# A head's mean taken out of the recurrence's values while they are turned into rows

## What is computed

```python
def rwkv7_scan(r, w, k, v, a, b):
    def step(state, inp):
        r_t, w_t, k_t, v_t, a_t, b_t = inp
        sa = jnp.einsum('bhvk,bhk->bhv', state, a_t)
        state = (state * w_t[:, :, None, :]
                 + sa[..., None] * b_t[:, :, None, :]
                 + v_t[..., None] * k_t[:, :, None, :])
        return state, jnp.einsum('bhvk,bhk->bhv', state, r_t)
...
    y = rwkv7_scan(r, decay, k, v, -kk, kk * a)
    mu = jnp.mean(y, axis=-1, keepdims=True)
    var = jnp.mean(jnp.square(y - mu), axis=-1, keepdims=True)
    y = ((y - mu) * lax.rsqrt(var + GN_EPS)).reshape(bsz, s, c) * gn_w + gn_b
    bonus = jnp.sum(r * k * r_k, axis=-1, keepdims=True) * v
    return (y + bonus.reshape(bsz, s, c)) * g
```

## Time and profile before

| | |
|---|---|
| median of 3 runs | 2821.63 us (2818.89 to 2824.79) |
| the profiled execution | 2820.33 us, span of its profile 2818.5 us |
| PE busy | 2771.2 us, 98% of the span |
| PEld / DVE / ACT / POOL busy | 2434.1 / 2023.7 / 1364.0 / 479.3 us |
| chain that ended last | PE 90%, DVE 5%, ACT 2%, POOL 1% of the span |
| granted TensorE clock | 0.997 of full speed |
| DMA | 474.65 MB, mean 168 GB/s |

### The profile page before, as it was taken

One profiled execution on the slowest core, in us unless ns is written; L12 is line 12 of the kernel. 1 busy time (PEld: TensorE's weight loads), 2 busy tenths in 40 slices (PEclk: granted clock), 3 DMA queues, 4 the chain that ended last, 5 costly groups with the idle time before them and its releaser, 6 DMA issues.

```text
span 2818.5 us, 42260 instructions
## 1 busy us (share of the span) xinstructions
PE 2771.2 (98%) x16660; PEld 2434.1 (86%) x16660; DVE 2023.7 (72%) x3102; ACT 1364.0 (48%) x2051; POOL 479.3 (17%) x526
## 2 busy tenths in 40 slices
PE   8999999999999999999999999999999999999998
PEld 7888888888888888888888888878998888888887
DVE  7987797776776666656657888878677777667655
ACT  6453455455555445434435545434454444444434
POOL 2211011110111111001102635421111111001101
PEclk9999999999999999999999999999999999999999
DMA  6444333455555555555556534221365555555555
GB/s 227 162 160 159 121 116 132 145 191 188 193 187 190 192 191 191 192 190 193 188 183 199 177 124 133 92 76 53 120 202 191 191 192 189 193 188 194 189 180 164
DMA packets 133396, 474.65 MB, mean 168 GB/s; under 512 B 14800, under 2 KB 15056, under 8 KB 132944
## 3 DMA queue, kind: packets, MB, share of 16 engines
q1 hardware_dynamic: 133200, 471.96, 50.3%
HBM read 469.80 MB, written 2.10 MB: 167 GB/s over the span
## 4 chain that ended last, share of the span: by engine, by line
PE 90%; DVE 5%; ACT 2%; POOL 1%; issue 1%; DMA 0%; SPq 0%; DVEq 0%; ACTq 0%; POOLq 0%
PE ps L899 90%; DVE U L1869 1%; DVE ringl L1869 1%; POOL U L2551 1%; ACT high L1409 1%; PE ps L902 1%; POOL U L2624 0%; ACT U L1409 0%; DVE U L1878 0%; DVE xT L1869 0%; DMA xT<-in_x_dram 0%; DVE hx L1869 0%; DVE U L2067 0%; ACT hr L1409 0%; DVE U L1875 0%
## 5 line engine op out<-in xcount | busy, mean ns | idle before, releaser
L899 PE MATMUL ps<-hr,high 128*128 128x512 f32 x4672 | 1491.4, 397 | 11.8 <-DVE ringl L1869 10.8
L1869 DVE TENSOR_TENSOR ringl<-ring,high 128x1024 fp32r<-128x1024 f32 x888 | 1082.6, 1221 | 435.1 <-ACT high L1409 434.6
L1409 ACT ACTIVATE high<-ring 128x1024 fp32r<-128x1024 f32 x888 | 915.6, 1033 | 601.6 <-PE ps L899 590.7
L899 PEld LDWEIGHTS ps<-hr,ringl 128*128 128x128 f32 x4672 | 879.2, 188 | 192.5 <-issue 1.4
L899 PE MATMUL ps<-hr,ringl 128*128 128x256 f32 x4672 | 924.3, 279 | 0.0
L899 PEld LDWEIGHTS ps<-hr,high 128*128 128x128 f32 x4672 | 717.6, 188 | 21.0 <-issue 15.1
L899 PE MATMUL ps<-yur,high 128*128 128x512 f32 (+1 forms) x2432 | 682.9, 370 | 3.8 <-DVE xT L1869 2.2
L2551 POOL TENSOR_TENSOR U<-U,rs 128x256 f32<-128x256 f32 x292 | 264.5, 906 | 1688.3 <-DVE U L1869 1668.8
L899 PEld LDWEIGHTS ps<-yur,ringl 128*128 128x128 f32 x2176 | 400.0, 188 | 79.6
L1409 ACT ACTIVATE U<-ps 128x256 f32<-128x256 f32 (+3 forms) x481 | 172.8, 371 | 592.0 <-PE ps L899 567.6
L899 PE MATMUL ps<-yur,ringl 128*128 128x256 f32 x2176 | 429.9, 279 | 0.0
(11 more groups left out here) (178 smaller groups left out, 1250.2 us busy)
## 6 DMA issues: line engine op xcount, KB each, us to landing
ring<-in_w_dram SPq DMA_DIRECT2D x862, 512.0 KB, 3.3
ring<-in_w_dram SPq DMA_DIRECT2D x48, 256.0 KB, 3.3
xT<-in_x_dram SPq DMA_DIRECT2D x3, 512.0 KB, 8.1
out_dram<-hx SPq DMA_DIRECT2D x3, 512.0 KB, 2.7
cst<-in_cst_dram SPq DMA_DIRECT2D x1, 1374.5 KB, 12.5
yT<-in_lora_dram SPq DMA_DIRECT2D x1, 1024.0 KB, 7.4
xT<-in_x_dram SPq DMA_DIRECT2D x2, 256.0 KB, 4.5
U<-in_lora_dram SPq DMA_DIRECT2D x1, 512.0 KB, 5.4
```

What stands on the lines that cost most here:

```text
L899: return e.matmul(out, l, r, start=start, stop=stop)
L1409: return e.activation(out, i, ACT.Copy, scale=scale)
L1869: return e.tensor_tensor(out, a, b, op)
```

## The change

`cen` is a new constant of 128 columns: the identity less 1/64 on the two 64x64 blocks on the diagonal. In the rows step, v's two chunks are multiplied by `cen` as the moving side instead of transposed, which gives rows with the mean over each head's 64 channels taken out; B's and K's rows are made with transposes instead of with matmuls. ACT squares each chunk of the result directly from PSUM, then copies it. The step `mean` is gone on TensorE, ACT and DVE. In `RECUR` the step `mean` goes and the ACT cost of `o0` and `o1` is 0.6 instead of 0.35. Each stream takes one PSUM bank fewer per q.

```diff
--- before.py
+++ after.py
@@ -50,9 +50,9 @@
          ("kk", ("PE", 0.45), ("DVE", 0.42), ("ACT", 1.7)), ("nrm", ("DVE", 3.1)), ("em", ("DVE", 1.2)), ("exp", ("ACT", 2.9)),
          ("rk", ("PE", 0.45), ("DVE", 0.42)), ("ar", ("DVE", 1.8)), ("rows", ("PE", 0.9), ("ACT", 1.1)),
          ("p1", ("PE", 0.9), ("DVE", 1.4)), ("p2", ("PE", 0.9), ("+DVE", 1.4))] + INVERSE \
-    + [("G0", ("PE", 0.45), ("ACT", 0.35)), ("sa0", ("PE", 0.45), ("ACT", 0.45)), ("o0", ("PE", 1.35), ("ACT", 0.35), ("DVE", 0.4)),
-       ("G1", ("PE", 0.7), ("ACT", 0.35)), ("sa1", ("PE", 0.45), ("ACT", 0.45)), ("o1", ("PE", 1.1), ("ACT", 0.35)),
-       ("mean", ("PE", 0.45), ("DVE", 0.45), ("ACT", 0.45)), ("var", ("PE", 0.45), ("ACT", 1.8)), ("fin", ("DVE", 2.2), ("+POOL", 2.9))]
+    + [("G0", ("PE", 0.45), ("ACT", 0.35)), ("sa0", ("PE", 0.45), ("ACT", 0.45)), ("o0", ("PE", 1.35), ("ACT", 0.6), ("DVE", 0.4)),
+       ("G1", ("PE", 0.7), ("ACT", 0.35)), ("sa1", ("PE", 0.45), ("ACT", 0.45)), ("o1", ("PE", 1.1), ("ACT", 0.6)),
+       ("var", ("PE", 0.45), ("ACT", 1.8)), ("fin", ("DVE", 2.2), ("+POOL", 2.9))]
 ROPE1 = (("DVE", 2.9),)
 ROPE = (("PE", 0.9), ("DVE", 2.1))
 
@@ -71,7 +71,7 @@
 def layout():
     at, out = 0, {}
     for name, n in [
-        ("ones", 128), ("norm1", 16), ("eps", 1), ("ident", 128), ("bones", 128), ("SU", 128), ("utri", 128), ("MC", 4 * 64), ("B8", 128), ("E8", 8),
+        ("ones", 128), ("norm1", 16), ("eps", 1), ("ident", 128), ("bones", 128), ("cen", 128), ("SU", 128), ("utri", 128), ("MC", 4 * 64), ("B8", 128), ("E8", 8),
         ("zero", 128), ("causal", 128), ("causalT", 128),
         ("head", 2), ("R2", 128), ("cos1", 256), ("sin1", 256), ("inv2", 1), ("cmpmask", 32), ("anyv", 2),
         ("eps128", 1), ("eps64", 1), ("zc", 1), ("halfpi", 1),
@@ -1253,7 +1253,7 @@
                 AR, Bt, Kt = w["AR"], w["B"], w["K"]
                 P1, P2, Vp, SAp, G, Br, Kr, S = [w[n] for n in ("P1", "P2", "Vp", "SAp", "G", "Br", "Kr", "S")]
                 X, XT, Y = w["X"], w["XT"], w["Y"]
-                E, F, yc = w["E"], w["rk"], w["X"].rearrange("p a b -> p (a b)")[:, 0:256]
+                E, F = w["E"], w["rk"]
                 sq = w["X"].rearrange("p a b -> p (a b)")[:, 256:512]
                 for q in range(s, 8, STREAMS):
                     pcs = slice(128 * q, 128 * q + 128)
@@ -1278,10 +1278,10 @@
                     yield "rk"
                     b = take(ac, "kr", q)
                     e.wait_ge(vc_.sem, vc_.after("ab", q))
-                    tr(ps[b][:, 0:128], v[:, 0:128])
-                    tr(ps[b][:, 128:256], v[:, 128:256])
-                    mm(ps[b][:, 256:384], Bt[:, 0:128], ident, True, True)
-                    mm(ps[b][:, 384:512], Kt[:, 0:128], ident, True, True).then_inc(pc.sem, pc.inc("rows", q))
+                    mm(ps[b][:, 0:128], v[:, 0:128], C("cen"), True, True)
+                    mm(ps[b][:, 128:256], v[:, 128:256], C("cen"), True, True)
+                    tr(ps[b][:, 256:384], Bt[:, 0:128])
+                    tr(ps[b][:, 384:512], Kt[:, 0:128]).then_inc(pc.sem, pc.inc("rows", q))
                     yield "rows"
 
                     for x, src in ((1, Bt), (2, Kt)):
@@ -1329,12 +1329,8 @@
                                 t = mm(shaped(ps[b][:, 0:128], 2, 64), r_, both_heads, r_ is Br, r_ is Kr)
                             t.then_inc(pc.sem, pc.inc("S", q))
                         yield f"o{c}"
-                    b = take(vc_, "mean", q)
-                    e.wait_ge(ac.sem, ac.after("yc", 1, q))
-                    mm(ps[b][:, 0:256], bones, yc, True, True).then_inc(pc.sem, pc.inc("mean", q))
-                    yield "mean"
                     b = take(ac, "rs", q)
-                    e.wait_ge(ac.sem, ac.after("sq", q))
+                    e.wait_ge(ac.sem, ac.after("sq", 1, q))
                     mm(ps[b][:, 0:256], bones, sq, True, True).then_inc(pc.sem, pc.inc("var", q))
                     yield "var"
 
@@ -1814,14 +1810,12 @@
                         yield f"sa{c}"
                         b, _ = rota.take()
                         e.wait_ge(pc.sem, pc.after("o", c, q))
-                        copy(yc[:, 128 * c:128 * c + 128], ps[b][:, 0:128]).then_inc(ac.sem, ac.inc("yc", c, q))
+                        cs = slice(128 * c, 128 * c + 128)
+                        e.activation(sq[:, cs], ps[b][:, 0:128], ACT.Square).then_inc(ac.sem, ac.inc("sq", c, q))
+                        copy(yc[:, cs], ps[b][:, 0:128]).then_inc(ac.sem, ac.inc("yc", c, q))
                         if c == 0:
                             rota.take()
                         yield f"o{c}"
-                    rota.take()
-                    e.wait_ge(vc_.sem, vc_.after("mean", q))
-                    e.activation(sq, yc, ACT.Square).then_inc(ac.sem, ac.inc("sq", q))
-                    yield "mean"
                     b, _ = rota.take()
                     e.wait_ge(pc.sem, pc.after("var", q))
                     e.activation(rs, ps[b][:, 0:256], ACT.Sqrt, scale=1.0 / 64, bias=C("eps64"))\
@@ -2461,10 +2455,6 @@
                             e.wait_ge(pc.sem, pc.after("S", q))
                             stt(S, ps[b][:, 0:128], em[:, 3:4], bones, MUL, MUL).then_inc(vc_.sem, vc_.inc("S", q))
                             yield "o0"
-                    b, _ = rota.take()
-                    e.wait_ge(pc.sem, pc.after("mean", q))
-                    stt(yc, ps[b][:, 0:256], -1.0 / 64, yc, MUL, ADD).then_inc(vc_.sem, vc_.inc("mean", q))
-                    yield "mean"
                     rota.take()
                     e.wait_ge(ac.sem, ac.after("rs", q))
                     e.reciprocal(rs, rs).then_inc(vc_.sem, vc_.inc())
@@ -2715,6 +2705,7 @@
     put("ident", np.eye(128, dtype=np.float32))
     put("ones", np.ones((128, 128), np.float32))
     put("bones", (I // 64 == J // 64).astype(np.float32))
+    put("cen", ((I == J) - (I // 64 == J // 64) / 64).astype(np.float32))
     put("utri", (I <= J).astype(np.float32))
     put("SU", (I < J).astype(np.float32))
     put("head", np.stack([i < 64, i >= 64], 1).astype(np.float32))
```

## The result

| | before | after |
|---|---|---|
| median | 2822.93 us (2818.89 to 2824.79, 4 runs) | 2835.59 us (2833.27 to 2838.53, 4 runs) |
| ratio after to before | | 1.0048, 95% interval 1.0033 to 1.0063 |
| profiled execution, span | 2820.33 us, 2818.5 us | 2838.53 us, 2836.7 us |
| PE busy | 2771.2 us | 2782.1 us |
| DVE / ACT busy | 2023.7 / 1364.0 us | 2020.8 / 1357.3 us |

What follows compares the result with a forecast made beforehand. TensorE was taken as the bound. Matmuls 4.4, waits 0.7 + 0.6 + 0.6, less 0.2 for constants, took 6.1 us off the profiled 2820.3; with 1.3 added for the median, 2815.5 us, range 2809 to 2822.

Steps and rivals of the forecast that it cites:

- New order: Planner's re-placing of side steps in the recurrence: taken at 0, with 3 us either way.
- The slower rival: New order puts square roots and reciprocals ahead of main evacuations, up to 1.6 us each; about 2828 us, chance 0.06.
- Idle time of 10 us and more there would speak for the bad order: Sign to check: TensorE's idle time from 1960 to 2040 us, expected near 4.5 us instead of 6.2.
- Eight matmuls at 0.55, 4.4 us: Removed fp32 128x256 products of the mean on TensorE: 4.4 us saved, ends 3.4 and 5.4.
- The idle 0.46 and 0.22 us at the means: TensorE waits in front of the means of q = 6 and q = 7: both go, 0.7 us saved.
- The 0.61 us wait behind DVE's subtraction: At q = 7 TensorE waits for a bank whose evacuation queues behind DVE's mean instruction: goes, 0.6 us saved.
- The 1.31 us wait: At 2011.15 us main work waits for the last head's halves behind POOL: half taken, 0.6 us, ends 0 and 1.31.
- The 1.59 us wait: At 2006.77 us, behind DVE's reciprocal, the square root and its table load: expected to stay.
- The four shifts of 2.8 us: Shorter chain in each of a stream's four runs: last one may end 11 us earlier, worth only the waits removed.
- Swap of the rows: Rows step, two matmuls and two transposes exchanged one for one on TensorE: price 0, bounds 0.7 us either way.
- The longer bank hold: Square ahead of ACT's copy holds the PSUM bank 0.27 us longer: 0, hidden by 1.43 us slack; 2.2 us at most.
- Constants: 128 more columns, 64 KB, in the table's second load delay the loads behind it: 0.2 us lost, ends 0 and 0.2.

Runs made afterwards that it cites:

- old_places: The changed kernel with the planner's old costs and the removed step mean kept as an empty step, so all places are as before; 2821.50 us, ratio 0.9993.
- old_sums_new_costs: The kernel before with only the planner's ACT cost of o0 and o1 raised from 0.35 to 0.6; 2836.25 us, ratio 1.0048.
- the two price runs: mean_twice and rows_swapped, each one edit to the kernel before with every place kept; 2825.41 us and 2822.47 us.
- mean_twice: The kernel before with the product of the mean issued twice, 8 more products of 256 columns; 2825.41 us, ratio 1.0012.
- after_old_costs: The changed kernel with the planner's ACT cost of o0 and o1 back at 0.35, step mean still out of the plan; 2831.32 us, ratio 1.0033.
- after_kept_busy: The changed kernel with nine unread fp32 products ahead of the 3.90 us TensorE wait in q = 7's inverse; 2833.05 us, ratio 1.0039.
- plan_a: The changed kernel with three planner durations altered (lw DVE 1.35, sa1 PE 0.59, fin POOL 2.32); 2817.08 us, ratio 0.9982.
- after_filled: The changed kernel with nine unread products ahead of the 3.90 us wait and two ahead of each other inverse step of q = 6 and 7; 2837.62 us, ratio 1.0050.
- rows_swapped: The kernel before with only the rows step changed: values by products with the identity, keys by transposes; 2822.47 us, ratio 0.9998.

## Why the prediction was wrong

**The step that failed is "New order".** It took the planner's reaction at 0 with 3 us either way, from the waits that stood in the trace. Measured, it is 14.1 us (old_places to after), and 13.5 us with the arithmetic of before (old_sums_new_costs). The reasoning went wrong at one sentence: "one more or one fewer is as likely". The waits of the earlier trace rows belong to one plan, which is among the best of its neighbours; another draw is likelier to be worse. A small edit redraws the whole plan from the first changed step on, and the price of a redraw is the spread over plans (the planned ends of the 1200 altered tables reach from 2769 to 2818), not the size of one wait. The prediction also says that the trace can't show the new order. The kernel's own planner can.

**The slower rival had the right sign and the wrong mechanism.** It put 2828 us on square roots and reciprocals ahead of main evacuations. The waits of after on such evacuations (releaser DVE xT) are 0.60 to 0.61 us and five in number, 3.0 us in all against 2.2 before. The loss lies mostly in the inverses' small products and the waits before them, which no rival named. Its chance of 0.06 was too small for an order that had not been looked at. Its time of about 2828 us is below all runs of after (2833.27 to 2838.53), so the sign is all that it had right.

**Idle time was read as if it were the whole loss.** "Idle time of 10 us and more there would speak for the bad order": from 1960 to 2040 us PE idles 2.40 + 5.27 = 7.67 us in after, less than that, and the order was bad. A stretch at half the clock counts as busy. The clock column and the count in brackets have to be read with the busy time.

**The arithmetic's terms**, by old_places and the two price runs:
- Eight matmuls at 0.55, 4.4 us: too large. Up to 1948 us, where six are removed, old_places has gained 2.44 us (3.29 less the 0.85 of its start), 0.41 for each, which is the cheap price of 0.43 and not the middle. At q = 6 nothing is gained. At q = 7 it is 1.2 us, with the product and its wait of 0.22 in it. A second product in each place costs the same 0.42 in the full part and nothing at q = 6 (mean_twice).
- The idle 0.46 and 0.22 us at the means: both rows are gone. The 0.46 brought no time, since the new wait of 1.74 us at 1956.08 stands in its place, as shown above. The earlier trace rows could not show that: without the rows of 0.96, 0.60 and 0.15 us, the end of q = 6 looked as if the mean alone held it up.
- The 0.61 us wait behind DVE's subtraction: predicted gone, still there with 0.60. It ends with the same kind of evacuation; the instruction queued ahead of it was not what made it late.
- The 1.31 us wait: predicted to halve, still 1.33. The 1.59 us wait stayed, as said. (The prediction counts 1.61 us among four "main waits"; its own second paragraph calls that row an attention product.)
- The four shifts of 2.8 us, 11 us in all, didn't come. The last square root stands at 1999.15 in old_places and 2003.58 before, 4.4 us earlier, no more than everything else there. The steps keep their places among main blocks, so a shorter chain only waits longer for its turn.
- Swap of the rows: 0, confirmed. The Squares: 16 of 278 ns, as expected.
- The longer bank hold was not measured by itself. The Trainium skill ("Perfetto Trace Analysis", section "Matmuls") wants independent groups of matmuls to rotate through PSUM banks, so that the evacuation of one overlaps the next. The prediction gave 2.2 us, from its own rows, as the price if the longer hold spoilt that. No sign of it is seen: with the longer hold in the kernel the first six removed products give 0.41 us each, where six added ones cost 0.37 each; a loss of 0.27 at each q would leave a gain of 0.1.
- Constants: 0.2 us can't be told from the 1.1 us behind and 0.8 us ahead that after and old_places, with the same constants, have near 1584 us.

Together 3.6 us in the stage where 6.3 were forecast (6.1 and the 0.2 of the constants), and 1.3 between the medians. Why the medians show less is open. The profiled execution of old_places is the second fastest of ten, and its granted clock over the whole kernel is 0.998, as in the fastest alone; it is 0.997 in the other eight.

**Where the rest of the gain went.** In its profiled execution old_places is 4.42 us ahead at 2006.73 and 1.8 at the end: 2.6 us are given back in the output projection, as the last section tells. That belongs to the pair of executions that were profiled, not to the change.

## What to carry to other kernels

Where a planner orders the work, an edit has two prices: that of the instructions, and that of the new plan, which can be several times as large with either sign. Hold the plan still (an empty step in the old place, the old costs) to measure the first, and run the planner on the edited table before predicting the second. A plan that stands among the best of its neighbours (as this one did) is likely to lose by a redraw, so search for a new one: here, three numbers of a table apart, the same arithmetic takes 2835.6 or 2817.1 us.

## What the runs showed of the hardware

**The clock falls under small products, not only behind a long wait.** With nine filling products the wait was 0.78 us and the clock still went to 0.50 among the 128x64 products; with two more ahead of each following step it stayed at 1.00 up to 2000 us. In after it came back shortly before 1980 us (0.53 from 1970 to 1980, 1.00 from 1980 on), after 128x128 products had come in from 1975.02 on.

**The output projection runs at one of two rates**, from one execution to another. Its pairs start 0.68 us apart in the profiled execution of before (timeline of PE):

```profile
2074.24 0.39 PE L899 MATMUL ps<-yur,ringl 128*128 128x256 f32 x2
2074.92 0.39 PE L899 MATMUL ps<-yur,ringl 128*128 128x256 f32 x2
2075.60 0.39 PE L899 MATMUL ps<-yur,ringl 128*128 128x256 f32 x2
```

and 0.71 us apart in mean_twice:

```profile
2073.80 0.40 PE L899 MATMUL ps<-yur,ringl 128*128 128x256 f32 x2
2074.51 0.40 PE L899 MATMUL ps<-yur,ringl 128*128 128x256 f32 x2
2075.22 0.40 PE L899 MATMUL ps<-yur,ringl 128*128 128x256 f32 x2
```

The granted clock is 1.00 in both. Over the 70 us of this part it makes 2.6 us. The executions of before, after_old_costs, after_kept_busy, plan_a and after_filled were profiled at the short distance, after, old_places and the seven others at the long one. It is not the order of the program: rows_swapped has the plan of before and ran at the long distance. The row of 2011.15 comes 1.19 us earlier there than in before, as the whole stage does, and by 2074 us its products come 1.26 us later, so the difference begins behind that row. What chooses it stays open. It is one reason for not reading a difference of 2 us between single profiles.
